# First scale and shift made in two ways, the input turned early, and eight projection groups between the modulation groups

## The chip, the core and the metric

One core of a Trainium2 chip runs the whole program. The metric is the device time of one execution in microseconds. Engines: TensorE (PE) multiplies, VectorE (DVE) and ScalarE (ACT) work elementwise, GpSimd (POOL) does small work and issues some transfers, SyncE (SP) only issues transfers, in order, and waits on semaphores in between.

## The reference

Two transformer blocks on 256 tokens of width 2048, in float32. The part at issue is the start of the first block:

```python
cond = jax.nn.silu(c)
mod = cond @ w_ada[l] + b_ada[l]
sh1, sc1, gt1, sh2, sc2, gt2 = [m[:, None, :] for m in jnp.split(mod, N_MOD, axis=-1)]
h = rms_norm(x, g_pre_mix[l]) * (1.0 + sc1) + sh1
y = token_mixing(h, w_in[l], b_in[l], ...)     # p = h @ w_in + b_in, then three branches and gates
```

`w_ada` is 2048 x 12288 and `c` one row of 2048, so `mod` is a product of one row with a 96 MB matrix. `w_in` is 2048 x 9216. The branches (spatial gating, attention with ALiBi, pooling) and twelve gate chunks are made from `p`.

## The kernel before

**Streams.** Every weight matrix is cut into groups of 1 MB (128 partitions x 4 k-tiles x 512 columns). SyncE loads them into four slots `w_raw`. For each projection group ScalarE makes a high part (`split`, L783), VectorE the rest (`split`, L1244), and TensorE does three matmuls per tile with them (`three`, L1974 to 1978): 24 matmuls of 512 columns per group for the first projection (`rows_group`, L2065). Group s uses slot s % 4; the load of group s+4 is issued when TensorE has finished group s (`pe_used`, L343 to 345). Four groups make one chunk of 512 output columns; VectorE evacuates it (`evac`, L1325).

**Front.** `N_FRONT` = 32 groups of `w_ada` (16 for the scale, 16 for the shift) go through the same four slots. TensorE multiplies them with `cond` broadcast over 128 columns (`mods`, L2041 to 2052), so every partition holds the same row of `mod`. VectorE adds the bias row, makes h1 from x in token rows (L1288 to 1303), and TensorE turns h1 (L2058 to 2061) with ScalarE and VectorE making the high and low part of `h1T` (L789, L1258). Only then the 72 groups of the first projection begin.

**Side work.** The later modulations (36 groups in this stage, `A_IN`) are summed on VectorE instead: `ada_group` (L1310) multiplies four k-tiles of 128x512 by a scalar of `cond` and adds them up; after four groups TensorE adds over the partitions (`product`, L2092) and VectorE adds the result to `mod_cols` (L1344). The loads use two slots `ada1`. On VectorE `to` (L1334) runs side group r ahead of the split of step 2(r+1); SyncE issues the load of side group r+2 in its step 2(r+1), behind the weight load of that step (L346 to 349). The branches' small steps lie between the groups by hand-written step numbers, on each engine for itself (`to(n)` runs the queue up to group n), and the bank of each turn or product follows a fixed order (`ROUNDS1`).

## Time and profile before

| | |
|---|---|
| median of 3 runs | 3100.39 us (3099.34 to 3111.67) |
| profiled execution, its own time | 3099.43 us |
| span of its trace | 3097.7 us |
| mean granted TensorE clock | 0.982 |
| TensorE matmul busy | 2986.2 us (96%) |
| VectorE busy | 1816.6 us (59%) |
| ScalarE busy | 1261.5 us (41%) |
| moved from and to memory | 215 GB/s over the span |

Times in the rows are microseconds from the span's start, and those marked ns nanoseconds. A matmul in float32 (the modulation products) leaves two records, one of the split type or a transpose leaves one. The page's part 4 gives the chain of work that ended last, followed back; its shares tell which engine the end depended on. Busy shares are means over stages with different limits, so each stage is read by itself.

### The profile page before, as it was taken

What the parts mean: (1) busy time and instruction counts of PE and PEld (TensorE: products, weight loads), DVE (VectorE), ACT (ScalarE), POOL (GpSimd) and SP (SyncE); (2) the same over time, 40 slices, a digit from 0 to 9 for tenths busy, and PEclk for the clock granted to TensorE, in tenths of its full rate; (3) what the DMA queues carried; (4) which work ended last, traced back from release to release, by engine and by line L of the source; (5) the groups of instructions that cost most, each with busy time, mean ns of one, the idle gap of its engine ahead of it and who ended that gap; (6) DMA issues with size and microseconds to landing.
All of it is one profiled execution on the core that took longest, in us unless ns stands there. A gap on an engine that the chain in (4) does not pass through costs nothing.

```text
span 3097.7 us, 43203 instructions
## 1 busy us (share of the span) xinstructions
PE 2986.2 (96%) x18072; PEld 2589.7 (84%) x18072; DVE 1816.6 (59%) x1777; ACT 1261.5 (41%) x1207; POOL 325.2 (10%) x465
## 2 busy tenths in 40 slices
PE   8899999997999999999898999998999999999998
PEld 3488777876999999888687888877889999999886
DVE  1376777787677775544455437654555555555444
ACT  0133555435444454344433434334444343443343
POOL 1000000001000000000104908720000000000000
PEclk9899999998999999999898999999999999999999
DMA  9777777885666654555546652225654555555554
GB/s 363 275 274 269 278 282 287 303 349 200 245 228 234 231 217 178 205 217 204 193 151 190 212 209 85 91 75 192 242 187 180 192 196 195 190 191 208 211 210 170
DMA packets 109853, 666.49 MB, mean 215 GB/s; under 512 B 23472, under 2 KB 25680, under 8 KB 33296
## 3 DMA queue, kind: packets, MB, share of 16 engines
q1 hardware_dynamic: 101584, 626.96, 55.8%
q0 software_dynamic: 8144, 37.74, 3.3%
q8 instruction: 94, 1.54, 0.2%
q14 instruction: 31, 0.25, 0.0%
HBM read 647.26 MB, written 17.39 MB: 215 GB/s over the span
## 4 chain that ended last, share of the span: by engine, by line
PE 91%; DVE 3%; DMA 2%; ACT 2%; issue 1%; POOL 0%; SPq 0%; DVEq 0%; ACTq 0%; POOLq 0%
PE acc L1976 27%; PE acc L1978 27%; PE acc L1977 27%; PE ms L2050 3%; PE tp L2025 1%; DVE w_lo L1244 1%; DMA ada<-ada_stream 1%; DMA w_raw<-w_stream 1%; PE ms L2435 0%; PE acc L2474 0%; DMA w_raw<-ada_stream 0%; PE acc L2464 0%; ACT w_hi L783 0%; PE ms L2434 0%; ACT bias_rows L914 0%
## 5 line engine op out<-in xcount | busy, mean ns | idle before, releaser
L1244 DVE TENSOR_TENSOR w_lo<-w_raw,w_hi 128x2048 fp32r<-128x2048 f32 x484 | 1110.0, 2303 | 731.9 <-ACT w_hi L783 713.1
L783 ACT ACTIVATE w_hi<-w_raw 128x2048 fp32r<-128x2048 f32 x484 | 922.8, 1915 | 986.1 <-DMA w_raw<-w_stream 983.8
L1976 PE MATMUL acc<-h2T_hi,w_lo 128*128 128x256 f32 x2816 | 783.0, 278 | 0.0
L1977 PE MATMUL acc<-h2T_lo,w_hi 128*128 128x256 f32 x2816 | 782.0, 278 | 0.0
L1978 PE MATMUL acc<-h2T_hi,w_hi 128*128 128x256 f32 x2816 | 781.9, 278 | 0.0
L1977 PEld LDWEIGHTS acc<-h2T_lo,w_hi 128*128 128x128 f32 x2816 | 530.7, 188 | 0.0
L1978 PEld LDWEIGHTS acc<-h2T_hi,w_hi 128*128 128x128 f32 x2816 | 530.3, 188 | 0.0
L1976 PEld LDWEIGHTS acc<-h2T_hi,w_lo 128*128 128x128 f32 x2816 | 529.7, 188 | 0.0
L1976 PE MATMUL acc<-w_hi,hid_lo 128*128 128x512 f32 x704 | 275.1, 391 | 6.1 <-DVE w_lo L1244 6.1
L1977 PE MATMUL acc<-w_lo,hid_hi 128*128 128x512 f32 x704 | 274.5, 390 | 0.0
L1978 PE MATMUL acc<-w_hi,hid_hi 128*128 128x512 f32 x704 | 274.4, 390 | 0.0
L1976 PE MATMUL acc<-w_hi,h1T_lo 128*128 128x512 f32 x576 | 231.1, 401 | 1.5 <-DVE h1T_lo L1258 1.5
L1978 PE MATMUL acc<-w_hi,h1T_hi 128*128 128x512 f32 x576 | 225.5, 392 | 0.0
L1977 PE MATMUL acc<-w_lo,h1T_hi 128*128 128x512 f32 x576 | 225.5, 391 | 0.0
L1319 DVE SCALAR_TENSOR_TENSOR mod_sum<-ada,cond,mod_sum 128x512 f32<-128x512 f32 x240 | 180.3, 751 | 42.9 <-DMA ada<-ada_stream 35.9
L1976 PEld LDWEIGHTS acc<-w_hi,hid_lo 128*128 128x128 f32 x704 | 132.5, 188 | 34.8 <-DVE w_lo L1244 7.4
L1977 PEld LDWEIGHTS acc<-w_lo,hid_hi 128*128 128x128 f32 x704 | 132.6, 188 | 27.6
L1978 PEld LDWEIGHTS acc<-w_hi,hid_hi 128*128 128x128 f32 x704 | 132.5, 188 | 27.5
L1976 PE MATMUL acc<-w_hi,nT_lo 128*128 128x512 f32 x320 | 127.7, 399 | 9.3 <-DVE w_lo L1244 9.3
L1976 PEld LDWEIGHTS acc<-w_hi,h1T_lo 128*128 128x128 f32 x576 | 108.7, 189 | 29.0 <-issue 4.5
L1978 PEld LDWEIGHTS acc<-w_hi,h1T_hi 128*128 128x128 f32 x576 | 108.7, 189 | 23.5
L1977 PEld LDWEIGHTS acc<-w_lo,h1T_hi 128*128 128x128 f32 x576 | 108.8, 189 | 21.5
(517 smaller groups left out, 3962.0 us busy)
## 6 DMA issues: line engine op xcount, KB each, us to landing
w_raw<-w_stream SPq DMA_DIRECT2D x484, 1024.0 KB, 4.8
ada<-ada_stream SPq DMA_DIRECT2D x64, 1024.0 KB, 6.9
w_raw<-ada_stream SPq DMA_DIRECT2D x32, 1024.0 KB, 4.9
g_dram<-gates_out SPq DMA_DIRECT2D x12, 512.0 KB, 7.1
gates_in<-g_dram POOLq DMA_DIRECT2D x12, 512.0 KB, 6.2
bias_rows<-b_in POOLq DMA_DIRECT2D x18, 256.0 KB, 6.1
x_res<-x POOLq DMA_DIRECT2D x2, 2048.0 KB, 12.2
g_dram<-gate_stage SPq DMA_DIRECT2D x8, 512.0 KB, 6.1
```

The costliest lines, as they stand in the source:

```text
L783: sc.activation(whi[:, s % 4], raw[:, s % 4], ACT.Copy).then_inc(hi_made, 1)
L1244: v.tensor_tensor(wlo[:, s % 4], raw[:, s % 4], whi[:, s % 4].bitcast(F32), ALU.subtract).then_inc(lo_made, 1)
L1319: chain(v.scalar_tensor_tensor(macc[:], slots[b][:, q], cond[:, k:k + 1], macc[:], ALU.mult, ALU.add))
L1976: mm(o, sl, mh, start=start, stop=False, skip_group_check=share)
L1977: mm(o, sh, ml, start=False, stop=False, skip_group_check=share)
L1978: return mm(o, sh, mh, start=False, stop=stop, skip_group_check=share)
L2025: ins = tr(t[0:w, c:c + n], src, ident[0:n, 0:n])
L2050: ins = mm(ms[n][:], cond[:, k:k + 1].to_broadcast([P, P]), raw[:, g, q], start=k == 0, stop=k == KD - 1)
```

## The change

- The 16 scale groups stay matmuls on TensorE, through four slots of their own (`ada_first`). The 16 shift groups are summed on VectorE with `ada_group` and the two slots `ada1`. SyncE issues scale and shift loads in turn, and eight projection loads (chunks 0 and 1 alternating by k-group) among them.
- x is normalized in place on VectorE (by rstd alone), turned in eight rounds on TensorE and copied by ScalarE to `xT`, while the modulations still run.
- For each quarter c of the width, ScalarE copies the scale row out of its bank, TensorE turns it to columns and adds the shift's column product in the same bank (`first_product`); VectorE adds the biases (now loaded as columns); ScalarE writes `h1T_hi` from `xT` with scale and bias as columns, VectorE the same value into `x_mod` and the difference into `h1T_lo` (`first_rows`).
- TensorE runs projection group c of chunk 0, two scale groups, group c of chunk 1, one scale group, the product, one scale group (`first_mods`, `rows_group`).
- The 36 side groups stand at the steps 10, 12, ... 70 and 17, 27, 37, 47, 57 (`SIDE`) instead of 2, 4, ... 72. The branches' steps and products move by one or two groups; of the early save of modulation rows only the first 16 rows remain.
- The broadcast loads of b_ada (2 MB) and g_pre_mix (1 MB) are replaced by loads as columns (24 KB).

```diff
+N_EARLY = 8
+SIDE = sorted(list(range(10, 71, 2)) + [17, 27, 37, 47, 57])
...
-            for j in range(4):
-                load(j, a["ada_stream"][j])
-            with sp.Fori(1, N_FRONT // 4) as i:
-                for j in range(4):
-                    sp.wait_ge(ada_used, (i - 1) * 4 + j + 1)
-                    load(j, row(a["ada_stream"], i * 4 + j))
-            for j in range(4):
-                sp.wait_ge(ada_used, N_FRONT - 3 + j)
-                load(j, a["w_stream"][j])
...
+            def first(p):
+                n, h = divmod(p, 2)
+                src = a["ada_stream"][h * 4 * GK + n]
+                if h:
+                    if n >= 2:
+                        sp.wait_ge(mod_used, n - 1)
+                    load_ada(ada1, n % 2, src)
+                else:
+                    if n >= 4:
+                        sp.wait_ge(ada_used, n - 3)
+                    sp.dma_start(adaf[n % 4][:].rearrange("p k c -> p (k c)"), src).then_inc(first_in[n % 4], 16)
+            def early(s):
+                if s >= 4:
+                    sp.wait_ge(pe_used, s - 3)
+                load(s % 4, a["w_stream"][s % 2 * 4 + s // 2])
+            for p in range(N_FRONT):
+                first(p)
+                if p >= 7 and p % 4 == 3:
+                    early(p // 4 - 1)
+            early(N_EARLY - 1)
             for j in range(2):
+                sp.wait_ge(mod_used, A_FIRST - 1 + j)
                 load_ada(ada1, j, a["ada_stream"][N_FRONT + j])
-            for s in range(G_IN1):
+            for s in range(4, G_IN1):
                 sp.wait_ge(pe_used, s + 1)
                 load(s % 4, a["w_stream"][s + 4])
-                r = s // 2 - 1
-                if s % 2 == 0 and s and r + 2 < A_IN:
-                    sp.wait_ge(mod_used, r + 1)
-                    load_ada(ada1, r % 2, a["ada_stream"][N_FRONT + r + 2])
+                for r in range(A_IN - 2):
+                    if SIDE[r] == s:
+                        sp.wait_ge(mod_used, A_FIRST + r + 1)
+                        load_ada(ada1, r % 2, a["ada_stream"][N_FRONT + r + 2])
...
-            fetch("rows1", row1[:].rearrange("p a b -> p (a b)"), bc(a["b_ada"][0]))
-            fetch("rows1", rowT1[:], bc(a["g_pre_mix"]))
             fetch("ident", ident[:], a["ident"])
+            fetch("first_cols", bcol, a["b_ada_first"])
+            fetch("first_cols", pcol, a["g_pre_mix"])
...
-            squares(lambda k: x[:, k], lambda k: h1[:, k], P, (0, 1)).then_inc(sem("ssq"), 1)
-            split()
-            split()
-            turns_hi(h1T[0], KD)
+            xflat = xT[:].rearrange("p k s -> p (k s)")
+            squares(lambda k: x[:, k], lambda k: xflat[:, k * D:(k + 1) * D], P, (0, 1)).then_inc(sem("ssq"), 1)
+            for r in range(KD // 2):
+                act.wait_ge(tp_full, r + 1)
+                sc.activation(xflat[:, r * C:(r + 1) * C], tp[r % 2][:], ACT.Copy).then_inc(tp_free[r % 2], 1)
+            for c in range(4):
+                act.wait_ge(ada_used, GK * (c + 1))
+                sc.activation(rowc[:], ms[c % 2][:], ACT.Copy).then_inc(sem("row_copied"), 1)
+                act.wait_ge(sem("mod_evac"), c + 1)
+                for k in range(GK * c, GK * c + GK):
+                    ins = sc.activation(h1T[0][:, k], xT[:, k], ACT.Identity, scale=acol[:, k:k + 1], bias=scol1[:, k:k + 1])
+                ins.then_inc(sem("h1_hi"), 1)
+                split()
+                split()
...
-            dve.wait_ge(sem("ld_rows1"), 32)
-            for n in range(2 * D // C):
-                c = slice(n % 4 * C, (n % 4 + 1) * C)
-                r = row1[:, n // 4, c]
-                dve.wait_ge(ada_used, (n + 1) * 4)
-                chain(v.tensor_tensor(r, ms[n % 2][:], r, ALU.add))
-                dve.sem_inc(sem("mod_evac"), 1)
-                if n < 4:
-                    chain(v.scalar_tensor_tensor(r, r, 1.0, rowT1[:, c], ALU.add, ALU.mult))
-                    if n == 0:
-                        rstd_wait()
-                for t in range(TT):
-                    if n < 4:
-                        chain(scaled(h1[:, t, c], x[:, t, c], t, r))
-                    else:
-                        v.tensor_tensor(h1[:, t, c], h1[:, t, c], r, ALU.add).then_inc(sem("h1"), 1)
-            split()
-            split()
-            turns_lo(h1T, KD)
...
+            def first_shifts(g0, g1):
+                for n in range(g0, g1):
+                    ada_group(ada1, macc1[n // GK % 2], n % GK)
+            def first_rows(c):
+                dve.wait_ge(sem("shifts"), c + 1)
+                k = slice(GK * c, GK * c + GK)
+                b = ms[c % 2][:].rearrange("p (f s) -> p f s", s=P)
+                v.tensor_tensor(scol1[:, k], b[:, :, 1], bcol[:, 1, k], ALU.add)
+                chain(v.tensor_tensor(acol[:, k], b[:, :, 0], bcol[:, 0, k], ALU.add))
+                chain(v.scalar_tensor_tensor(acol[:, k], acol[:, k], 1.0, pcol[:, k], ALU.add, ALU.mult))
+                dve.sem_inc(sem("mod_evac"), 1)
+                if c == 0:
+                    for b in range(2):
+                        dve.wait_ge(tp_free[b], KD // 4)
+                for i in range(GK):
+                    kk = GK * c + i
+                    ins = v.tensor_scalar(xm[:, i], xT[:, kk], acol[:, kk:kk + 1], scol1[:, kk:kk + 1], ALU.mult, ALU.add)
+                chain(ins)
+                dve.wait_ge(sem("h1_hi"), c + 1)
+                v.tensor_tensor(h1T[1][:, k], xm[:], h1T[0][:, k].bitcast(F32), ALU.subtract).then_inc(sem("h1"), 1)
+            dve.wait_ge(sem("cond"), 1)
+            first_shifts(0, GK)
+            rstd_wait()
+            for t in range(TT):
+                v.tensor_scalar(x[:, t], x[:, t], rstd[:, t:t + 1], None, ALU.mult).then_inc(sem("xn"), 1)
+            dve.wait_ge(sem("ld_first_cols"), 32)
+            for c in range(4):
+                if c < 3:
+                    first_shifts(GK * (c + 1), GK * (c + 1) + 2)
+                first_rows(c)
+                split()
+                if c < 3:
+                    first_shifts(GK * (c + 1) + 2, GK * (c + 2))
+                split()
+            dve.wait_ge(sem("h1"), 4)
...
                 while m.n <= s:
-                    r = m.n // 2 - 1
-                    if m.n % 2 == 0 and r < A_IN:
+                    if m.n in SIDE:
+                        r = SIDE.index(m.n)
                         ada_group(ada1, macc1[r // 4 % 2], r % 4)
                     split()
-                    if m.n % 4 == 2 and m.n < 4 * (BRANCH + 12) + 6:
+                    if m.n == N_EARLY + 1:
+                        evac(0)
+                    elif m.n % 4 == 2 and m.n < 4 * (BRANCH + 12) + 6:
...
+            def first_product(c):
+                pe.wait_ge(sem("row_copied"), c + 1)
+                for f in range(4):
+                    tr(ms[c % 2][:, f * P:(f + 1) * P], rowc[:, f * P:(f + 1) * P], ident[:])
+                pe.wait_ge(mod_acc, c + 1)
+                for f in range(4):
+                    ins = mm(ms[c % 2][:, f * P + 1:f * P + 2], macc1[c % 2][:, f * P:(f + 1) * P], ones[:], start=True, stop=True)
+                ins.then_inc(sem("shifts"), 1)
...
+            first_mods(0, 0, GK)
+            pe.wait_ge(sem("ones"), 1)
+            pe.wait_ge(sem("ld_ident"), 16)
+            pe.wait_ge(sem("xn"), TT)
+            for k in range(KD // 2):
+                turn([(x[:, t, (2 * k + q) * P:(2 * k + q + 1) * P], q * S + t * P) for q in range(2) for t in range(TT)])
+            first_product(0)
+            first_mods(1, 0, 2)
+            chunks.add(2)
+            for c in range(4):
+                pe.wait_ge(sem("h1"), c + 1)
+                rows_group(bank(0), h1T, c)
+                if c < 3:
+                    first_mods(c + 1, 2, GK)
+                rows_group(bank(1), h1T, c)
+                if c < 2:
+                    first_mods(c + 2, 0, 1)
+                if c < 3:
+                    first_product(c + 1)
+                if c < 2:
+                    first_mods(c + 2, 1, 2)
```

## Rows read from the trace of the kernel before

**Rows 1.** Page, part 4: the chain that ended last, share by engine.
```profile
PE 91%; DVE 3%; DMA 2%; ACT 2%; issue 1%; POOL 0%; SPq 0%; DVEq 0%; ACTq 0%; POOLq 0%
```
**Rows 2.** Windows: length, busy (records) by engine, granted clock, DMA share, GB/s.
```profile
core 0: us, PE busy (x) PEld busy (x) DVE busy (x) ACT busy (x) POOL busy (x), PEclk, DMA share, GB/s
25.00:50.00 25.00, 23.04 (x53) 10.09 (x54) 5.78 (x8) 0.00 (x0) 0.00 (x0) 1.00 0.99 397
...
125.00:150.00 25.00, 16.29 (x60) 13.06 (x61) 20.83 (x20) 7.37 (x9) 5.00 (x6) 0.66 0.65 232
```
**Rows 3.** Timeline of TensorE, front: start, length, instruction, [idle before, releaser].
```profile
30.66 92.97 PE L2050 MATMUL ms<-w_raw,cond 128*128 128x512 f32 x216 [0.26 <-DMA w_raw<-ada_stream]
123.47 1.04 PE L2025 MATMUL tp<-ident,h 128*128 128x128 f32 x8
130.95 1.94 PE L2025 MATMUL tp<-ident,h 128*128 128x128 f32 x8 [6.45 <-DVE h1T_lo L1258]
...
139.54 0.77 PE L1976 MATMUL acc<-w_hi,h1T_lo 128*128 128x512 f32 x1 [1.46 <-DVE h1T_lo L1258]
...
144.37 0.44 PE L1978 MATMUL acc<-w_hi,h1T_hi 128*128 128x512 f32 x1
```
**Rows 4.** Timeline of SyncE's queue: issues of weight and side loads.
```profile
185.67 6.72 SPq L322 DMA_DIRECT2D w_raw<-w_stream  x2
...
229.61 0.43 SPq L338 DMA_DIRECT2D ada<-ada_stream  x1
...
298.67 5.77 SPq L322 DMA_DIRECT2D w_raw<-w_stream  x2
...
310.19 5.77 SPq L322 DMA_DIRECT2D w_raw<-w_stream  x2
...
492.02 0.33 SPq L322 DMA_DIRECT2D w_raw<-w_stream  x1
...
498.11 5.77 SPq L322 DMA_DIRECT2D w_raw<-w_stream  x2
...
570.37 11.21 SPq L322 DMA_DIRECT2D w_raw<-w_stream  x3
```
**Rows 5.** All waits of TensorE from 180 to 600: us, times, longest.
```profile
PE tp L2025 <- DVEq L1348: 0.8, 1, 0.8
```
**Rows 6.** Groups by line, 140 to 600: busy us, mean ns, idle before.
```profile
L783 ACT ACTIVATE w_hi<-w_raw 128x2048 fp32r<-128x2048 f32 x75 | 143.3, 1912 | 88.9 <-DMA w_raw<-w_stream 88.8
...
L840 ACT ACTIVATE pool_y<-ms,pool_scale 128x256 f32<-128x256 f32 x4 | 1.7, 470 | 13.5 <-PE ms L2123 13.5
...
L1244 DVE TENSOR_TENSOR w_lo<-w_raw,w_hi 128x2048 fp32r<-128x2048 f32 x75 | 173.4, 2316 | 32.4 <-ACT w_hi L783 25.8 <-DVE mod_sum L1319 2.2 <-DVE mod_cols L1347 0.2
L1319 DVE SCALAR_TENSOR_TENSOR mod_sum<-ada,cond,mod_sum 128x512 f32<-128x512 f32 x135 | 101.5, 752 | 38.6 <-DMA ada<-ada_stream 34.8
...
L1440 DVE TENSOR_SCALAR scores<-scores,row_inv 128x256 f32<-128x256 f32 x8 | 2.8, 354 | 0.3
...
L1347 DVE TENSOR_TENSOR mod_cols<-mod_cols,tp 128x4 f32<-128x4 f32 x9 | 1.4, 151 | 0.0
...
L1377 DVE TENSOR_SCALAR proj<-proj,sumsq 128x512 f32<-128x512 f32 x2 | 1.0, 488 | 0.1
```
**Rows 7.** DMA issues up to 8 us: size, median us from issue to landing.
```profile
w_raw<-ada_stream SPq DMA_DIRECT2D x4, 1024.0 KB, 10.4
x_res<-x POOLq DMA_DIRECT2D x1, 2048.0 KB, 14.6
```
**Rows 8.** Windows of 4 us in the output projection, columns as in rows 2.
```profile
684.00:688.00 4.00, 1.87 (x7) 1.51 (x8) 3.93 (x4) 1.91 (x1) 0.00 (x0) 0.90 0.97 410
688.00:692.00 4.00, 4.00 (x14) 3.19 (x13) 3.78 (x5) 1.92 (x1) 0.00 (x0) 0.68 0.48 178
```
**Rows 9.** Side loads (tile ada) from 130 to 600: issue to landing.
```profile
DMA to landing us min/median/max: 6.7/7.0/10.6
```
**Rows 10.** Timeline of VectorE: the split behind a late side group.
```profile
239.73 2.29 DVE L1244 TENSOR_TENSOR w_lo<-w_raw,w_hi 128x2048 fp32r<-128x2048 f32 x1
```
**Rows 11.** Chain of waits in order of time, output projection.
```profile
667.29 9.57 DMA ada<-ada_stream
```

More of the change, by code:

```diff
@@ L197, in block_program @@
         gb1 = [u(f"gates_in{j}", [P, TT, C], 32 + 4 * j) for j in range(3)]
-        h1 = u("h1", [P, TT, D], 56)
+        adaf = [u(f"ada_first{j}", [P, GK, C], 40 + 8 * j) for j in range(4)]
+        xT = u("xT", [P, KD, S], 72)
+        xm = u("x_mod", [P, GK, S], 100)
+        rowc = u("row_copy", [P, C], 88.5)
         tril = u("tril", [P, P], 88)
-        row1, rowT1 = u("row1", [P, 2, D], 32), u("rowT1", [P, D], 48)
         y3T = [u("y3T_hi", [P, 3, 4, S], 64, F32R), u("y3T_lo", [P, 3, 4, S], 76, F32R)]
@@ L297, in block_program @@
         ada_in = [sem("ada_in0"), sem("ada_in1")]
+        first_in = [sem(f"first_in{i}") for i in range(4)]
         mod_used, mod_acc, mod_sum = sem("mod_used"), sem("mod_acc"), sem("mod_sum")
@@ L884, in _ @@
                     w = (n % 2 + 1) * P
+                    if (hp, n) == (2, 0):
+                        to(b + 4)
+                        r = R1["mod_rows1"]
+                        act.wait_ge(tp_full, r + 1)
+                        chain(sc.activation(modr1[0:D // P], tp[r % 2][0:D // P, 0:P], ACT.Copy))
+                        act.sem_inc(tp_free[r % 2], 1)
+                        act.sem_inc(sem("mod_rows"), 1)
                     to(b + 5 + 2 * n)
@@ L2038, in _, with first_mods @@
             pe.wait_ge(sem("cond"), 1)
-            modc = Tally()
-            def mods():
-                for n in range(2):
-                    if not modc.early(2):
-                        pe.wait_ge(sem("mod_evac"), modc.n - 1)
-                    for g in range(4):
-                        pe.wait_ge(raw_in[g], (modc.n + 1) * 16)
-                        for q in range(GK):
-                            k = g * GK + q
-                            ins = mm(ms[n][:], cond[:, k:k + 1].to_broadcast([P, P]), raw[:, g, q], start=k == 0, stop=k == KD - 1)
-                        ins.then_inc(ada_used, 1)
-                    modc.add()
-            mods()
-            with engine_loop(pe, N_FRONT // 8 - 1, (modc, 2)) as i:
-                mods()
-            pe.wait_ge(sem("ld_ident"), 16)
-            for n in range(4):
-                pe.wait_ge(sem("h1"), 2 * n + 2)
-                for k in range(2 * n, 2 * n + 2):
-                    turn([(h1[:, t, (2 * k + q) * P:(2 * k + q + 1) * P], q * S + t * P) for q in range(2) for t in range(TT)])
-            turned()
-            sums = Tally()
+            def first_mods(c, g0, g1):
+                if c >= 2 and g0 == 0:
+                    pe.wait_ge(sem("mod_evac"), c - 1)
+                for g in range(g0, g1):
+                    n = c * GK + g
+                    pe.wait_ge(first_in[n % 4], (n // 4 + 1) * 16)
+                    for q in range(GK):
+                        k = g * GK + q
+                        ins = mm(ms[c % 2][:], cond[:, k:k + 1].to_broadcast([P, P]), adaf[n % 4][:, q], start=k == 0, stop=k == KD - 1)
+                    ins.then_inc(ada_used, 1)
+            def first_product(c):
[6 more added lines that the diff above has]
+                ins.then_inc(sem("shifts"), 1)
             def rows_group(b, xT, g):
@@ L2073, in rows_group @@
                 end_group(ins)
+            first_mods(0, 0, GK)
[19 more added lines that the diff above has]
+                    first_mods(c + 2, 1, 2)
+            sums = Tally()
+            sums.add(GK)
             def to(s):
@@ L2126, in _ @@
             pe.wait_ge(sem("ones"), 1)
-            to(7)
-            product(0)
-            to(9)
+            to(10)
             pe.wait_ge(sem("sguw_m"), 1)
@@ L2142, in _ @@
             to(15)
-            product(1)
-            to(16)
+            product(0)
+            to(18)
             pe.wait_ge(sem("y_sgu"), 1)
@@ L2152, in _ @@
             pooled(0)
-            to(19)
+            to(21)
             pool_y(0)
-            to(20)
+            product(1)
+            to(22)
             pooled(1)
-            to(22)
+            to(23)
             pool_y(1)
-            to(23)
-            product(2)
             def qk_turn(hp):
@@ L2207, in _ @@
                     pv1(hp - 1, 3)
+                if hp == 1:
+                    product(3)
                 if hp == 3:
@@ L2212, in _ @@
                 to(b + 3)
+                if hp == 0:
+                    product(2)
                 if hp == 2:
+                    pe.wait_ge(sem("mod_cols"), 1)
+                    ring("mod_rows1")
+                    turn([(mcol[:, 0:D // P], 0)])
                     product(5)
@@ L2220, in _ @@
                     pv1(hp, n)
[L2221 to L2224 removed]
+                    if (hp, n) == (1, 1):
+                        product(4)
+                    if (hp, n) == (3, 1):
+                        product(7)
             to(64)
@@ L2228, in _ @@
             pv1(3, 3)
-            to(68)
-            pe.wait_ge(sem("mod_cols"), 1)
-            ring("mod_rows1")
-            turn([(mcol[:, 0:2 * D // P], 0)])
+            to(69)
+            product(8)
             to(71)
-            product(8)
             def merged_turns(n):
```

88 lines of the change are left out of this document (40 added, 48 removed).

## The prediction

> **What bounds the kernel now.** I read the page's chain of work first, because it tells whose time the end follows: TensorE holds 91% of it [rows 1]. So an edit is worth what it adds to or takes from TensorE's own queue. The stage windows come next [rows 2]: the first projections after 125 us are the one early stretch with TensorE far from full (16.3 of 25 us, granted clock 0.66). The timeline of TensorE says why [rows 3]. 216 records of the modulation matmuls (27 groups of 8 records) take 92.97 us, so one group of 1 MB costs 3.44 us; the DMA share is below full there, so TensorE sets this pace. Then the row is added, the input is turned, and the first projection matmul starts at 139.54. The transfer queue gives the ends of the projection groups, since each weight load is issued when a group ends [rows 4]: group 7 (the eighth) ends at 185.7, group 71 at 581.2. In between TensorE waited for others for 0.8 us in all [rows 5]. So TensorE has no slack here, and every new wait costs its full length.
>
> Call F(n) the end of group n. A projection group is 5.45 us where no small work lies between two ends: a pair of loads issued in 5.77 us, the second taking 0.33, is 5.44 apart [rows 4].
>
> **Part 1, the front.** What goes: 16 of 32 modulation groups leave TensorE (16 x 3.44 = 55.0 us), the 3 MB of broadcast rows leave the DMA engines, and the sixteen row operations on h1, hidden beside TensorE, go free. What comes: 16 multiply-add groups on VectorE, each 4 x 0.75 + 0.2 = 3.3 us [rows 6], and eight projection groups that now run inside the stage. I follow the new order by hand up to F(7).
>
> Arrivals: x lands at 16.7, and by then the transfer queue has had about four loads at half rate, the fourth at about 17.6 [rows 7]. After that one load per 2.64 us (1.05 MB at 397 GB/s) [rows 2]. The load order is scale, shift, scale, shift, so the fourth shift load (the eighth in the queue) lands at 28.2. VectorE needs 3.3 more (31.4), then normalizes x in place: two operations of 128x2048. No such row exists. From 354 ns at 256 and 488 ns at 512 elements [rows 6] the slope is 0.52 ns, so about 1.3 us each; at four times the 512 row it would be 2.0, so the bounds are 2.6 and 3.9 us. I take 2.6, since the two rows show a fixed part: 34.0.
>
> TensorE has been idle by then, so its clock is low. Eight rounds of transposes: 0.97 us each at the half clock and 0.52 at the full one [rows 3]. I take the half clock: 7.8, so 41.8. The row copy (1.2) and the first product (4 transposes and 4 one-column matmuls, taken as 2.0) bring 45.0. The next two modulation groups run cold at their start. After the gap of 6.45 us in the kernel before, matmuls were slow until 144.4, that is 4.9 us of work, half of it lost: 2.4 [rows 3]. So 45.0 + 6.9 + 2.4 = 54.3.
> The rows leave one thing open: there the slow rounds had waits of 0.65 us between them, here the eight follow each other, and if they count as work the clock could be back before the modulation groups, which takes up to 3.6 + 2.4 = 6.0 us off.
> The Trainium skill has a rule for it: TensorE: Matmul & The Clock Gate, Part 4 (PE-mode transpose), states that transposes do not count as TensorE being busy, so by it these 6.0 us are not to be had. The trace doesn't contradict it: all rounds after 130.95 stayed slow [rows 3].
>
> Now the step that repeats. Before projection group pair c can start, the product must reach VectorE: three small operations with their waits (0.9), ScalarE's four writes of h1T_hi (4 x 0.47 = 1.9), its split (1.9) and VectorE's split (2.3) [rows 6], in all 7.2 us with the signals. One modulation group (3.44) lies behind the product for c = 1 and 2, none for c = 3. So TensorE idles 3.8, 3.8 and 7.2 us. A gap of 2.4 us cost a clock of 0.90 and 0.68 in the next two 4 us windows [rows 8], 1.7 us of work lost; I take 1.6, 1.6 and, as after 6.45 us, 2.4. The sum:
> c = 0: 5.45 + 6.9 + 5.45 + 3.44 + product 1.5 + 3.44 = 26.2, from 54.4 to 80.5.
> c = 1: 3.8 + 1.6 + 26.2 = 31.6, to 112.1. c = 2: 3.8 + 1.6 + 5.45 + 6.9 + 5.45 + 1.5 = 24.7, to 136.8. c = 3: 7.2 + 2.4 + 10.9 = 20.5, to 157.3.
> Cover: the shift groups for the product of c = 3 are done about 13 us before it needs them and the loads never run dry after 50 us, so neither DMA nor VectorE's sums carry the path. F(7) comes at 157.3 in place of 185.7: a gain of 28.4 us, against the 8 groups of 5.45 (43.6) that one might book.
>
> **Part 2, the denser schedule.** Before, each of the 36 side groups (sums of the later modulations on VectorE, one every second step from 2) has its load issued four steps ahead. Now they stand at 10, 12, ... 70 and also at 17, 27, 37, 47, 57, still through two buffers. The load for side group r+2 is issued in the queue's step of side group r. So the one for step 18 is issued in step 16, after F(16); for 28 after F(26), and so at 38, 48, 58. Each step of VectorE runs side group, then split, in order; behind a late load its split waits, and behind that TensorE's group. The time from F(n) to the split: weight load issued first 0.4, landing 7.0 (6.7 to 10.6) [rows 9], sums 3.25, split 2.3, signal 0.1: 13.0 us. One such chain is in the trace: issued at 229.61, the split behind it started at 239.73 and took 2.29 [rows 4, 10]. From step n to n+2 TensorE has only group n+1 and what small work lies there.
> - Step 18: no small work is left between 16 and 18. 13.0 - 5.45 = 7.5 us.
> - Step 28: F(26) is 304.1, F(27) 310.2 (6.1), the product that moves there taken as 0.8 (eight records of a one-column matmul): 13.0 - 6.9 = 6.1.
> - Step 58: F(56) 492.0, F(57) 498.1: 13.0 - 6.1 = 6.9 [rows 4]. Step 38 as 58 (6.9), step 48 as 28 with one turn more (5.6).
> Steps 17, 27 and so on have their load three steps ahead: about 13 us against 12 to 15, at most 1 us, and it lies inside the wait that follows. Sum: 33.0 us. With it the clock falls again (gaps of 5 to 7 us, between those of 2.4 and 6.45): 2.0 us each, 10.0 for the five. Less the one wait of 0.8 [rows 5], which goes: 42.2 in all. Queued behind the waiting side group on VectorE are the split, the softmax and the bank's evacuation; they catch up before step 30.
> Edits at nothing: gelu, SGU and pooling two steps later in the same order; one row round (product and turn) earlier; no difference in work, all in TensorE's own queue as before. If a step is no longer covered, it is one small operation, below 1 us.
>
> **The sum** against the profiled execution: span 3097.7, time 3099.4, median 3100.4. 3099.4 - 28.4 + 42.2 = 3113.2; I say 3113.
>
> **Rivals.**
> A, the clock stays up: gaps and dense work in turn let it recover or never fall. For it: from 25 to 50 us TensorE was busy 23.0 of 25 us, so it had gaps, and the clock was 1.00 [rows 2]. Against: the gap of 2.4 us [rows 8]. The front gains 3.6 (rounds at 0.52) + 8.0, part 2 loses 10 less: 3113 - 21.6, about 3091.
> B, slower: the late side load lands later still. Three steps in a row now issue a weight load and a side load each. Where that happens in the kernel before, in the output projection, a side load took 9.6 us [rows 11]. If it does so here, five steps cost 2.6 more: 3126. It decides from about 7.5 us of landing, where the time passes 3116.
> C, faster: VectorE's lateness is absorbed (the load is out earlier than I read, or lands with VectorE ahead): part 2 costs nothing, 3071. Against: the order of the queue is written out, and TensorE had no slack [rows 5].
> D, the early groups don't go ahead: the queue stands at its in-order waits for VectorE's buffers, TensorE gets its eight groups only after the stage and F(7) stays near 185: 3141.
>
> **How the numbers follow.** Forecast 0.50 (own range 3103 to 3123), A 0.15, B 0.20, C 0.10, D 0.05. The range of 8 in 10 takes in A and B with the bounds of x (1.3 us) and of product and row copy (1 us each): 3088 to 3130. About 0.5%, 15.5 us, is what a measurement of this kernel can tell from no change: faster below 3085, slower above 3116. Faster is C and a tail of A: 0.12. Slower is B, D and some 0.3 of the forecast's own half: 0.40. The same 0.48.
>
> **What would show it.** F(7), read as the issue of the weight load for group 11: 157; at 146 A, at 180 D. TensorE's waits for w_lo at groups 18, 28, 38, 48, 58 of 5 to 7.5 us, each behind a side load of about 7.0 us; none is C, 9 us is B. Granted clock below 1.00 in the first 5 us after each. Between these places the groups keep 24.5 to 25 us per four. The sum is wrong at its root if the time between F(7) and F(71) is not near 438 us (395.5 before).

## The result, and the profile after

The changed kernel is slower, by a little more than a measurement of this kernel can tell from no change. One of the six runs before took 4337.0 us; the ratio is made without it.

| | before | after |
|---|---|---|
| median of the runs, us | 3099.9 (6 runs) | 3121.0 (6 runs, 3115.0 to 3125.9) |
| ratio after / before | | 1.0063, 95% interval 1.0051 to 1.0075 |
| span of the profiled execution, us | 3097.7 | 3118.4 |
| mean granted clock of TensorE | 0.982 | 0.975 |
| end of projection group 7, F(7), us | 185.7 | 156.5 |
| from there to the end of group 71, us | 395.6 | 444.8 |

The forecast was 3113, the range 3088 to 3130. The last two rows are the whole result: the front gained 29.2 us (forecast 28.4), the stretch behind it lost 49.2 (forecast 42.2), together +20.0 of the span's +20.7. They are read from SyncE's queue, as in [rows 4]; the columns are start, length and instruction. The first row is of the front and the last of the stage's end; those between stand around step 18.

```profile
123.45 49.75 SPq L330 DMA_DIRECT2D w_raw<-w_stream  x7
...
211.38 0.43 SPq L336 DMA_DIRECT2D ada<-ada_stream  x1
216.84 0.33 SPq L330 DMA_DIRECT2D w_raw<-w_stream  x1
...
232.61 0.33 SPq L330 DMA_DIRECT2D w_raw<-w_stream  x1
...
584.04 17.60 SPq L330 DMA_DIRECT2D w_raw<-w_stream  x4
```

Each weight load is issued when a group ends. The first row holds those behind groups 4 to 10: the last is issued at 123.45 + 49.75 - 0.33 = 172.9, and three groups of 5.45 ahead of it group 7 ended, at 156.5. The last row ends with the load behind group 71: 584.04 + 17.60 - 0.33 = 601.3. Group 18 ended at 232.61, 15.8 us after group 17, where a group alone takes 5.45.

The chain that ended last (page, part 4) has moved by 2% from TensorE to DMA and VectorE, against [rows 1]. The side loads hold 3% of it in the line list, where they held 1% before:

```profile
PE 89%; DVE 4%; DMA 4%; ACT 2%; issue 1%; SPq 0%; POOL 0%; DVEq 0%; ACTq 0%; POOLq 0%
PE acc L2028 27%; PE acc L2029 27%; PE acc L2030 27%; DMA ada<-ada_stream 3%; PE tp L2077 1%; DVE w_lo L1277 1%; PE ms L2101 1%; DVE mod_sum L1332 1%; DMA w_raw<-w_stream 1%; ACT w_hi L805 1%; PE ms L2509 0%; PE acc L2548 0%; PE acc L2538 0%; PE ms L2508 0%; ACT bias_rows L947 0%
```

All waits of TensorE from 160 to 620 us, where [rows 5] had a single 0.8 (columns: us in total, times, longest):

```profile
PE acc L2028 <- DVE w_lo L1277: 21.7, 7, 8.2
PE tp L2169 <- DVEq L1335: 6.8, 2, 3.7
PE ms L2245 <- ACT qkT L909: 5.0, 2, 2.5
```

Together 33.5 us. The side loads (tile ada) landed as before, so the loads are no slower as a rule (window 130 to 600 us); compare [rows 9]:

```profile
DMA to landing us min/median/max: 6.7/6.9/11.2
```

One close place in full, step 18: the side load was issued at 211.38 (above), VectorE stood idle for it and split behind it, and TensorE waited 8.21 us. Timelines of VectorE, then of TensorE:

```profile
219.41 3.11 DVE L1332 SCALAR_TENSOR_TENSOR mod_sum<-ada,cond,mod_sum 128x512 f32<-128x512 f32 x4 [7.28 <-DMA ada<-ada_stream]
222.67 4.49 DVE L1277 TENSOR_TENSOR w_lo<-w_raw,w_hi 128x2048 fp32r<-128x2048 f32 x2
```
```profile
225.02 0.79 PE L2028 MATMUL acc<-w_hi,h1T_lo 128*128 128x512 f32 x1 [8.21 <-DVE w_lo L1277]
```

From F(16) (211.0) to the split 222.67 are 11.7 us, to its end 225.0: 14.0, one more than the 13.0 of the forecast, since this load took 8.0 us to land. The granted clock (last columns: clock, DMA share, GB/s) falls in the gap and is back at 1.00 some four us after its end:

```profile
220.00:222.00 2.00, 0.00 (x0) 0.00 (x0) 1.89 (x4) 0.00 (x0) 0.00 (x0) 1.00 1.00 410
222.00:224.00 2.00, 0.00 (x0) 0.00 (x0) 1.85 (x2) 0.00 (x0) 0.00 (x0) 0.54 0.87 369
224.00:226.00 2.00, 0.98 (x2) 0.83 (x3) 2.00 (x2) 0.00 (x0) 0.00 (x0) 0.50 0.00 0
226.00:228.00 2.00, 2.00 (x6) 1.57 (x5) 1.97 (x3) 0.00 (x0) 0.00 (x0) 0.50 0.00 0
228.00:230.00 2.00, 2.00 (x8) 1.56 (x8) 1.93 (x3) 0.00 (x0) 0.00 (x0) 0.76 0.00 0
```

Busy time times the missing clock is the work lost: 0.98 x 0.5 + 2.0 x 0.5 + 2.0 x 0.24 = 2.0 us here. Summed so over all such windows from F(7) to F(71) it is 14.5 us after and none before. Waits 33.5 - 0.8 and clock 14.5 make 47.2 of the 49.2.

In the front, TensorE's timeline against [rows 3]:

```profile
35.65 6.89 PE L2077 MATMUL tp<-ident,x_res 128*128 128x128 f32 x32 [5.89 <-DVE x_res L1365]
...
45.36 10.15 PE L2101 MATMUL ms<-ada_first,cond 128*128 128x512 f32 x16
...
54.95 0.80 PE L2028 MATMUL acc<-w_hi,h1T_lo 128*128 128x512 f32 x1
```

and its waits for VectorE's split before the pairs c = 1, 2 and 3, two of 3.36 and one of 6.9:

```profile
PE acc L2028 <- DVE w_lo L1277: 13.6, 3, 6.9
```

### The profile page after: what moved, and what is told of

Same layout as the page of the kernel before. It is cut to its first block, busy times and chain, and to the rows that moved or that the text cites. A ratio compares the mean times of both kernels' runs of the same rounds, so it can differ in the third digit from the quotient of the medians.

```text
span 3118.4 us, 43026 instructions
## 1 busy us (share of the span) xinstructions
PE 2961.5 (95%) x17992; PEld 2585.1 (83%) x17992; DVE 1850.6 (59%) x1839; ACT 1271.1 (41%) x1227; POOL 325.2 (10%) x465
## 4 chain that ended last, share of the span: by engine, by line
PE 89%; DVE 4%; DMA 4%; ACT 2%; issue 1%; SPq 0%; POOL 0%; DVEq 0%; ACTq 0%; POOLq 0%
PE acc L2028 27%; PE acc L2029 27%; PE acc L2030 27%; DMA ada<-ada_stream 3%; PE tp L2077 1%; DVE w_lo L1277 1%; PE ms L2101 1%; DVE mod_sum L1332 1%; DMA w_raw<-w_stream 1%; ACT w_hi L805 1%; PE ms L2509 0%; PE acc L2548 0%; PE acc L2538 0%; PE ms L2508 0%; ACT bias_rows L947 0%
## 5 line engine op out<-in xcount | busy, mean ns | idle before, releaser
L1332 DVE SCALAR_TENSOR_TENSOR mod_sum<-ada,cond,mod_sum 128x512 f32<-128x512 f32 x300 | 225.3, 751 | 82.2 <-DMA ada<-ada_stream 73.0
L2028 PE MATMUL acc<-w_hi,h1T_lo 128*128 128x512 f32 x576 | 239.7, 416 | 35.4 <-DVE w_lo L1277 35.3
L2028 PEld LDWEIGHTS acc<-w_hi,h1T_lo 128*128 128x128 f32 x576 | 112.5, 195 | 68.4 <-issue 23.3
## 6 DMA issues: line engine op xcount, KB each, us to landing
ada_first<-ada_stream SPq DMA_DIRECT2D x16, 1024.0 KB, 10.1
```

The lines of the kernel that those rows point to most:

```text
L1332: chain(v.scalar_tensor_tensor(macc[:], slots[b][:, q], cond[:, k:k + 1], macc[:], ALU.mult, ALU.add))
L2028: mm(o, sl, mh, start=start, stop=False, skip_group_check=share)
```

## The experiments

Each kernel was timed beside the kernel before on the same chip. F(7) and F(71) are read as above; "waits" are TensorE's in the stage, from 160 to 620 us.

| kernel | median, us | before there | ratio, 95% | F(7) | F(7) to F(71) | waits |
|---|---|---|---|---|---|---|
| after | 3121.0 | 3099.9 | 1.0063 (1.0051 to 1.0075) | 156.5 | 444.8 | 33.5 |
| e1_spaced | 3077.7 | 3102.9 | 0.9919 (0.9901 to 0.9938) | 156.7 | 400.3 | 3.0 |
| e2_side_first | 3106.2 | 3102.9 | 1.0012 (1.0001 to 1.0024) | 153.4 | 432.9 | 25.3 |
| e3_old_front_close | 3135.8 | 3102.9 | 1.0098 (1.0078 to 1.0118) | 185.9 | 429.6 | 26.4 |
| e4_product_early | 3105.9 | 3102.9 | 1.0011 (0.9999 to 1.0022) | 140.0 | 442.9 | 31.3 |
| e5_filled | 3115.1 | 3101.3 | 1.0042 (1.0028 to 1.0055) | 151.8 | 447.0 | 27.3 |
| e6_spaced_early | 3063.9 | 3101.3 | 0.9881 (0.9866 to 0.9896) | 142.6 | 399.2 | 3.0 |
| e7_x_sooner | 3073.1 | 3101.3 | 0.9908 (0.9893 to 0.9923) | 145.8 | 400.8 | 3.0 |
| e8_rows_first | 3066.5 | 3100.0 | 0.9890 (0.9872 to 0.9907) | 141.7 | 404.2 | 3.0 |

**e1_spaced.** The new front is kept. Two side groups run inside it, two stand at step 8, and from 10 on they are two steps apart. The products 7 and 8 go back to their steps before, 63 and 71, and the columns of product 7 to step 66.

```diff
-SIDE = sorted(list(range(10, 71, 2)) + [17, 27, 37, 47, 57])
+SIDE = [-1, -1, 8, 8] + list(range(10, 73, 2))
...
-                for r in range(A_IN - 2):
-                    if SIDE[r] == s:
+                for r in {4: [0, 1], 6: [2], 7: [3]}.get(s, [s // 2 - 1] if s % 2 == 0 and 10 <= s <= 68 else []):
+                    if True:
...
+                else:
+                    for r in range(2):
+                        ada_group(ada1, macc1[0], r)
...
```

> The changed kernel with its new front kept and only the side groups spread out again: two run on VectorE while it waits for the last product of the front, two at step 8, and the rest every second step from 10 to 72 as in the kernel before. Theory L (the late load of the third of three close side groups costs the time, and the front by itself gains): F(7) stays at about 156.5 us, TensorE's waits for w_lo in this stage fall from 21.7 us to under 3, F(7) to F(71) goes back from 445 to about 396, and the whole is 29 us below the kernel before: about 3071. Rival V (VectorE and the DMA queue are too full once the shift sums are theirs, wherever the groups stand): the stage keeps most of its 49 us and the time stays above 3100. Rival G (the front's gain at F(7) is given back later, because the branches' steps come two groups later): F(7) at 156 but a total near 3100.

43 us below the changed kernel and 25 below before. All waits of the stage but one are gone, and that one has another cause:

```profile
PE tp L2082 <- DVE scores L1498: 3.0, 1, 3.0
```

The load behind group 7 and the last ones up to group 71 in SyncE's queue:

```profile
156.71 0.33 SPq L330 DMA_DIRECT2D w_raw<-w_stream  x1
...
546.17 11.21 SPq L330 DMA_DIRECT2D w_raw<-w_stream  x3
```

F(7) is the same (156.7), F(71) is at 557.1 in place of 601.3. So 44.5 of the 49.2 us hang on how close the side groups stand, and the front's 29 us are real: 29.0 less 4.7 is 24.3, and 25 were measured. Expected were 29 in all. What is missing is the one wait that is left, 3.0 us in group 49, and the 3.0 us of work lost by the clock around it: from F(44) to F(54) this kernel needs 68.4 us and the kernel before 62.4. Ahead of it, ScalarE's copy of the early modulation rows waits for their turn on TensorE until 404.9, behind group 47, and holds the next split. That turn is one of the steps that the change moved, counted at nothing in the forecast; no run moved it back, so this cause is read from the timelines and not tested.

**e2_side_first.** The changed kernel, with the two loads of a step in the other order.

```diff
                 sp.wait_ge(pe_used, s + 1)
-                load(s % 4, a["w_stream"][s + 4])
                 for r in range(A_IN - 2):
                     if SIDE[r] == s:
                         sp.wait_ge(mod_used, A_FIRST + r + 1)
                         load_ada(ada1, r % 2, a["ada_stream"][N_FRONT + r + 2])
+                load(s % 4, a["w_stream"][s + 4])
```

> The changed kernel with two lines of SyncE's loop exchanged: in a step that issues both, the side load goes ahead of the weight load. Theory L: the side load lands about 4.8 us after its issue instead of 7 to 8.2 and is issued 0.4 us sooner, so the third group of each of the five places comes 2.6 to 3.8 us sooner: 13 to 19 us less, 3102 to 3108. The weight load then lands late, at about 7 us, with three groups of slack. Rival V: VectorE's work is unchanged, so the time stays at 3121 within 3.

15 us below the changed kernel. The side loads landed 2.1 us sooner:

```profile
DMA to landing us min/median/max: 4.7/4.8/7.7
```

TensorE's waits in the stage fell by 8.2 (33.5 to 25.3) and the work lost by the clock from 14.5 to 10.1; the stretch is 11.9 shorter. That the late loads hold the five places is shown by this. Those five took 28.6 us to land in place of 37.7 (7.1 and 7.2 still at 38 and 58) and were issued 0.4 us sooner each. From F(n) to the end of the late split the five places took 55.4 us in place of 68.3, that is 12.9 less, about what the stretch lost. The profile is 3.1 us shorter in the front too, which the edit doesn't touch; that is a matter of the clock (last section), and as much was lost again behind F(71).

**e3_old_front_close.** The kernel before, its front untouched, with side groups at 17, 27 and 37 added in the same manner.

```diff
+SIDE = sorted(list(range(2, 67, 2)) + [17, 27, 37])
...
-                r = s // 2 - 1
-                if s % 2 == 0 and s and r + 2 < A_IN:
-                    sp.wait_ge(mod_used, r + 1)
-                    load_ada(ada1, r % 2, a["ada_stream"][N_FRONT + r + 2])
+                for r in range(A_IN - 2):
+                    if SIDE[r] == s:
+                        sp.wait_ge(mod_used, r + 1)
+                        load_ada(ada1, r % 2, a["ada_stream"][N_FRONT + r + 2])
...
-                    r = m.n // 2 - 1
-                    if m.n % 2 == 0 and r < A_IN:
+                    if m.n in SIDE:
+                        r = SIDE.index(m.n)
```

> The kernel before with one thing changed: its side groups stand at 2, 4, ... 66 and also at 17, 27 and 37, so that it has three of the five close places and the old front. Theory L: each place costs what it costs in the changed kernel, 8.8, 8.5 and 12.2 us between the same group ends, less what the last places of that kernel owe to its own order: 25 to 30 us, 3125 to 3130. Rival F (the places are late only because the new front leaves VectorE and the queue behind): no more than 5 us, 3100 to 3105.

33 us above before, with the old front: the cost doesn't need the new one. This is more than the 25 to 30 expected. By stretches: F(7) to F(24) +15.1, F(24) to F(34) +9.1, F(34) to F(44) +10.0, and from F(44) to F(67), where nothing was added, 143.0 as before. The place at 18 costs more than in the changed kernel (8.8). Here a turn stands ahead of group 17 on TensorE and needs a bank that VectorE frees only with the columns it makes after the late split of step 18 (`mod_cols(1)`), so not even group 17 runs beside the load:

```profile
PE tp L2026 <- DVEq L1349: 13.2, 1, 13.2
```

The profiled run was the slowest of four (3143.7 us against a median of 3135.8). The stage's +34.0 agrees with the median; the rest of the profile's difference is work lost by the clock behind F(71).

**e4_product_early.** The changed kernel; in the front, product(c+1) and its modulation group come ahead of the second projection group of c, so that one more group covers the hand-over to VectorE.

```diff
-                rows_group(bank(1), h1T, c)
-                if c < 2:
-                    first_mods(c + 2, 0, 1)
                 if c < 3:
                     first_product(c + 1)
+                rows_group(bank(1), h1T, c)
                 if c < 2:
-                    first_mods(c + 2, 1, 2)
+                    first_mods(c + 2, 0, 2)
```

> The changed kernel with one reordering in the front on TensorE: the product of quarter c+1 goes ahead of the second projection group of quarter c, so that this group and two modulation groups lie behind the product instead of one modulation group. Theory H (the hand-over of 7.2 us from product to the first projection group, uncovered by 3.8, 3.8 and 7.2 us, and the low clock behind it, set the length of the front): the waits at c = 1 and 2 go and the one at c = 3 falls to about 1.8 us, F(7) falls from 156.5 to about 141 and the whole by 15 us, to about 3106. Rival D (the loads set the front's length): the product then waits for the shift sums instead, F(7) stays above 152 and the time above 3117.

15 us below the changed kernel, and F(7) 16.5 earlier. The waits for VectorE's split in the front went from 13.6 to 3.0 us:

```profile
PE acc L2028 <- DVE w_lo L1277: 3.0, 2, 2.1
```

That is 10.6 us. Another 3.0 are clock behind the first product (the modulation row of 10.15 takes 7.1 here), which lie ahead of the edit and are scatter between profiles (last section). Behind the three gaps the clock had cost about 1.6 us each, 5 in all. Together that is 18.6, less some 2.4 of new short waits, most of them 0.69 us for the row copy before each later product. The stage behind it lost nothing of it (442.9).

**e5_filled.** The changed kernel with matmuls added that have no effect on the output, ahead of the groups for which TensorE waits.

```diff
+            pe.wait_ge(tp_free[0], KD // 4)
             for c in range(4):
+                for i in range([0, 4, 4, 8][c]):
+                    mm(tp[0][:], ident[:], xT[:, 2 * i:2 * i + 2].rearrange("p k s -> p (k s)"), start=True, stop=True)
                 pe.wait_ge(sem("h1"), c + 1)
...
+            to(17)
+            pe.wait_ge(tp_free[1], rounds.on_bank(1))
+            for i in range(8):
+                mm(tp[1][:], ident[:], wsT[:, 0:4].rearrange("p a b -> p (a b)"), start=True, stop=True)
             to(18)
```

> The changed kernel, with added matmuls that have no effect on the output: 4, 4 and 8 of them ahead of the first projection groups of c = 1, 2, 3 (each of 128x128 on 512 columns, at most 0.85 us cold), where TensorE idled 3 to 7 us for VectorE's split, and 8 ahead of group 18. Theory G (the low granted clock after a stall costs time of its own): the clock stays at 1.00 behind the four stalls, the stalls keep their ends, and the work behind them no longer runs at half speed: 1.6 + 1.6 + 2.4 us in the front and about 2.3 us at place 18, so about 8 us less than the changed kernel's 3121, about 3113, a ratio of about 1.004 to before; F(7) near 151 where it was 156.5. Rival N (the slow clock behind the stalls is hidden, or the added work itself runs past the stall's end): the ratio stays at 1.006 or rises to 1.008, F(7) stays at 156 or later.

Measured 6 us less, of 8 expected. In the front the price of the clock is shown clean: the pair c = 1 starts at 84.9 in both kernels, and the modulation row behind its first group at 92.08 in the changed kernel and at 90.44 here, 1.6 us sooner, the 1.6 of the forecast. The windows of the changed kernel, then of this one:

```profile
84.00:86.00 2.00, 1.10 (x4) 0.97 (x5) 1.97 (x3) 0.23 (x1) 0.00 (x0) 0.90 0.03 12
86.00:88.00 2.00, 2.00 (x6) 1.52 (x6) 1.78 (x4) 0.00 (x0) 0.00 (x0) 0.50 0.00 0
88.00:90.00 2.00, 2.00 (x8) 1.58 (x7) 1.93 (x3) 0.00 (x0) 0.00 (x0) 0.74 0.46 102
```
```profile
84.00:86.00 2.00, 2.00 (x8) 1.10 (x7) 1.97 (x3) 0.23 (x1) 0.00 (x0) 1.00 0.04 16
86.00:88.00 2.00, 2.00 (x11) 1.64 (x10) 1.78 (x4) 0.00 (x0) 0.00 (x0) 1.00 0.04 8
88.00:90.00 2.00, 2.00 (x11) 1.65 (x10) 1.93 (x3) 0.00 (x0) 0.00 (x0) 1.00 0.50 135
```

F(7) is 4.7 earlier (5.6 expected). At place 18 nothing was won: the added work ended at 219.0, TensorE stood 2.28 us all the same, and the clock fell to 0.53 and 0.62 in the next two windows of 2 us (222 to 226); a gap of that length can be enough, as in [rows 8]. The side load landed 1 us later than in the changed kernel, so group 18 took 16.5 us and not 15.8. The stage was 2.2 us longer than the changed kernel's in this profile (447.0), so that half of the front's gain was gone by F(71); the medians differ by 6.

**e6_spaced_early.** The edits of e1_spaced and e4_product_early together.

> The spaced side groups (e1_spaced, 25 us below before) and the product turned ahead of the second projection group of the front (e4_product_early, 16 us below the changed kernel) together. If the two are separate terms, as the sum has it (F(7) carries the one, F(7) to F(71) the other), they add: 3103 - 25 - 16 = 3062 us, ratio 0.987, F(7) near 140.5 and F(7) to F(71) near 396 to 399. If they share a resource (VectorE or the DMA engines, now 16 us earlier at the same rate of loads), the second part lengthens: side loads then find the queue less drained, and up to the 16 us come back: 3062 to 3078.

The best kernel of the study, 37 us below before. F(7) is 142.6 and the stretch 399.2: the stage keeps all its gain. The front keeps 14.1 of e4's 16.5. The two edits alone make 25 and 15 us, so 3 us less than their sum were measured, which the intervals don't tell from nothing. The two side groups that e1 put into the front are the edit that lies there, but this wasn't split further.

**e7_x_sooner.** As e6, and x is normalized one shift group sooner.

```diff
-            first_shifts(0, GK)
+            first_shifts(0, GK - 1)
             rstd_wait()
             for t in range(TT):
                 v.tensor_scalar(x[:, t], x[:, t], rstd[:, t:t + 1], None, ALU.mult).then_inc(sem("xn"), 1)
+            first_shifts(GK - 1, GK)
```

> As e6_spaced_early, and VectorE normalizes x after the third shift group of the front, not after the fourth. In the changed kernel the transposes of x began at 35.65 us, behind that fourth group's load. If the front's chain is the one told (shift load, sums, x, turns, product, projection), the turns begin about 5.3 us sooner (two loads of 2.64 us), at about 30.4, and what follows the product keeps its lengths: 5 us less than e6_spaced_early, about 3057. The limit: the fourth shift load is then also the last thing that the first product needs, at 33 to 37 us plus the product (1.5 us), and the turns take 5 to 7 us beside it; so 2 to 5 us less. If the front's end is set by the later loads, no difference (within 2 us).

5 us less were expected and 9 more measured: the expectation was wrong. The turns did begin at 29.8, and the product was done by 37.5, 7 us sooner. Yet VectorE took it up no sooner, since the sums of the next two shift loads stand ahead of it in its queue, each waiting for its load. VectorE in this kernel (the trace calls the columns of scale and shift conv_taps, and the last row is the first operation on the product):

```profile
37.70 0.49 DVE L1330 TENSOR_SCALAR mod_sum<-ada,cond 128x512 f32<-128x512 f32 x1 [4.87 <-DMA ada<-ada_stream]
38.22 2.33 DVE L1332 SCALAR_TENSOR_TENSOR mod_sum<-ada,cond,mod_sum 128x512 f32<-128x512 f32 x3
42.49 3.12 DVE L1332 SCALAR_TENSOR_TENSOR mod_sum<-ada,cond,mod_sum 128x512 f32<-128x512 f32 x4 [1.94 <-DMA ada<-ada_stream]
45.75 0.16 DVE L1347 TENSOR_TENSOR conv_taps<-ms,conv_taps 128x4 f32<-128x4 f32 x1
```

In e6 the last of these stands at 45.85. So TensorE's time from 37.5 on turned into a wait: 6.42 us before the first projection group, where e6 has 1.16. And the wait cost the clock. TensorE's first projection record in e7, then in e6:

```profile
52.62 0.76 PE L2034 MATMUL acc<-w_hi,h1T_lo 128*128 128x512 f32 x1 [6.42 <-DVE w_lo L1277]
```
```profile
52.71 0.47 PE L2033 MATMUL acc<-w_hi,h1T_lo 128*128 128x512 f32 x1 [1.16 <-DVE w_lo L1277]
```

Both start within 0.1 us; the modulation row behind the group starts at 60.92 and at 58.26. That difference, 2.7 us, is what a gap of 6.4 us costs in clock against one of 1.2, and it is most of the 3.2 us by which F(7) is later. The span grew by 9.0. Of this 4.2 lie behind F(71), where no edit is: the waits there are the same as in e6, but the work lost by the clock is about 30 us and not about 24. Why the clock is lower there stays open; the medians show the 9 us too.

**e8_rows_first.** As e7, and for c = 0 VectorE makes the product's operations and the first split ahead of those two sums.

```diff
-                if c < 3:
+                if 0 < c < 3:
                     first_shifts(GK * (c + 1), GK * (c + 1) + 2)
...
-                    first_shifts(GK * (c + 1) + 2, GK * (c + 2))
+                    first_shifts(GK * (c + 1) + (2 if c else 0), GK * (c + 2))
```

> As e7_x_sooner, and for c = 0 VectorE makes the product's three small operations, x_mod, h1T_lo and the first split before the sums of the next two shift loads, not behind them. In e7_x_sooner the product was turned by 37.5 us, 7 us earlier than in e6_spaced_early, and yet VectorE took it up at 45.75 in place of 45.85, since it stood behind two shift loads (sums at 37.70 and 42.49, each waiting for its load); TensorE's stall before the first projection group grew from 1.2 to 6.4 us and its clock fell, so that F(7) came at 145.8 and not 142.6. If that order is the cause of the miss, the product is taken up at about 37.8 here, the first projection group starts at about 45, and F(7) comes 5 to 8 us before that of e6_spaced_early (135 to 138): about 3057 us, ratio 0.986. The rival: the next loads, now freed later (VectorE sums shift loads 5 and 6 only from about 45 us), hold product(1) back, F(7) stays at 141 or later, and the time is e6_spaced_early's 3064 or above.

The order was what held e7 back: the product is taken up at 38.16 and the first pair starts at 45.02, 7.7 us sooner. But the rival is what came. The next shift loads are freed later, and the next product waits for them. VectorE's last shift sum and product of c = 1 in e8, then in e6:

```profile
70.25 3.11 DVE L1332 SCALAR_TENSOR_TENSOR mod_sum<-ada,cond,mod_sum 128x512 f32<-128x512 f32 x4 [2.61 <-DMA ada<-ada_stream]
73.51 0.16 DVE L1347 TENSOR_TENSOR conv_taps<-ms,conv_taps 128x4 f32<-128x4 f32 x1
```
```profile
68.44 3.11 DVE L1332 SCALAR_TENSOR_TENSOR mod_sum<-ada,cond,mod_sum 128x512 f32<-128x512 f32 x4 [2.02 <-DMA ada<-ada_stream]
71.70 0.16 DVE L1347 TENSOR_TENSOR conv_taps<-ms,conv_taps 128x4 f32<-128x4 f32 x1
```

In both VectorE waited for the load ahead of this product (2.61 and 2.02 us), so there the loads set the front, and the product comes 1.8 us later than in e6. From 46 to 50 us, with the buffers freed late, the DMA engines were busy for only half of the time in e8 and all of it in e6. The 7.7 us are gone. F(7) is 0.9 earlier, group 8 then waited 3.2 us for its accumulator bank, and F(71) is 4.2 later than in e6.

## Why the prediction was right, and where its steps were off

The sign, the size and both mechanisms were as forecast; the time was 8 us above, inside the range. The forecast drew its line for "slower" at 3116 and gave that 0.40, and 0.48 to no change that can be told; the median lies above the line.

**The front, step by step.** Turns start at 35.65 (34.0 for the end of x's two operations, which took 2.48 together and not 2.6; they began at 33.02, since the fourth shift load came about 1.4 us later than by the even rate of loads). The rounds took 6.9 and not 7.8. The two cancel: the modulation row after the product starts at 45.36 (forecast 45.0), the first projection group at 54.95 (54.4). The waits were 3.4, 3.4 and 6.9 (3.8, 3.8, 7.2), F(7) 156.5 (157.3). The clock's price of a short gap was taken from [rows 8] as 1.7 us over whole windows; busy time times the missing clock is 1.5 there, and e5 measured 1.6. Rival D would have had 185; it fell.

**The five close places.** TensorE's waits sum to 33.5 us (33.0 forecast), by place 8.2, 5.3, 6.5, 5.8 and 7.7 (7.5, 6.1, 6.9, 5.6 and 6.9). Two errors cancel in this. From F(n) to the end of the late split the five took 14.0, 13.3, 14.2, 13.0 and 13.8 us, 3.3 more in all than five times 13.0. And TensorE's own work in between was longer by 2.8 in all, most of it at 28 and 38, where a part of it ran at the low clock (1.7 us lost at 38).

Not foreseen was where the waits stand. Two of 2.5 us are for ScalarE's qk copy, behind groups 36 and 56, and 1.1 and 1.3 us for the splits of steps 27 and 47. They come from the side groups put in at 27, 37, 47 and 57. ScalarE at step 37: the gate of the bank before stands ahead of the copy, and waited for VectorE's evacuation, which stands behind the sum of step 37 and its split:

```profile
355.86 1.06 ACT L853 ACTIVATE gates_out<-gates_out 128x1024 f32<-128x1024 f32 x1 [10.05 <-DVE gates_out L1384]
...
357.35 0.39 ACT L909 ACTIVATE qkT<-tp 128x256 f32<-128x256 f32 x1
```
```profile
357.88 0.46 PE L2245 MATMUL ms<-qkT 64*128 64x128 f32 x2 [2.54 <-ACT qkT L909]
```

The step that was off is the one that said steps 17, 27 and so on cost at most 1 us "inside the wait that follows". They do lie inside it: all four stand between F(n) and the end of the late split, so the waits at the splits of 38 and 58 are 3.9 and 5.3 us and not 6.9. But they are longer than 1 us, two of them through a second engine, and at 38 they cost clock. In e2, where the side loads land sooner, the waits for the qk copy are gone.

**The mis-sized term is the clock.** Taken as 2.0 us for each place, 10.0 in all; it was 14.5, or 2.9 each. By place it was 2.0, 2.8, 4.7, 2.9 and 2.1. At 38 it fell twice, at the qk wait and at the split, which the forecast had as one gap; at 58, behind a qk wait of 2.4 us, it didn't fall until the split. This is the largest part of the 7 us by which the stretch was longer than forecast.

**By stretches**, each place's price after against before: F(7) to F(24) 8.8 us (forecast 9.5 for place 18), F(24) to F(34) 8.5 (8.1), F(34) to F(44) 12.2 (8.9), F(44) to F(54) 8.8 (7.6), F(54) to F(67) 9.9 (8.9); another 1.0 lies between F(67) and F(71). Place 38 is the outlier. Its side load took 8.2 us from issue (355.75) to the sum's start (363.96), yet its waits were 6.5, below the forecast's 6.9; what came on top is the clock, 4.7 in place of 2.0.

**The rivals.** A (the clock stays up) fell: 14.5 us were lost in the stage, and e5 and e7 show the price of single gaps (1.6 and 2.7). B (9.6 us of landing) fell as a rule, with a median of 6.9. But the five late loads took 8.0, 7.0, 8.2, 6.8 and 7.7, 7.5 on the mean, which is where the forecast said that the time would pass 3116. C (absorbed) fell, by the 33.5 us of waits.

**The rule on transposes.** The eight rounds now follow each other, which the rows of before left open. The granted clock:

```profile
38.00:40.00 2.00, 2.00 (x11) 1.57 (x9) 1.89 (x4) 1.39 (x3) 0.00 (x0) 0.50 1.00 422
40.00:42.00 2.00, 1.88 (x11) 1.33 (x10) 0.46 (x1) 1.39 (x4) 0.00 (x0) 0.69 1.03 434
42.00:44.00 2.00, 0.82 (x7) 0.59 (x8) 1.54 (x3) 1.49 (x3) 0.00 (x0) 1.00 1.00 422
44.00:46.00 2.00, 2.00 (x13) 1.84 (x12) 1.78 (x5) 0.00 (x0) 0.00 (x0) 0.66 1.02 430
46.00:48.00 2.00, 2.00 (x3) 0.67 (x2) 1.46 (x5) 1.83 (x4) 0.00 (x0) 0.50 1.01 426
```

It rose to full speed by 42 us, with nothing but transposes run since the gap that ended at 35.65; in e2_side_first and e4_product_early it was at 1.00 from 40 us on. The Trainium skill (TensorE: Matmul & The Clock Gate, Part 4, PE-mode transpose) says that a transpose does not count as TensorE being busy in the same way, and that the full clock doesn't come with it. The float32 transposes measured here disagree with that. The time nearly agreed all the same, and that was luck: in this execution the clock fell again by 46 us and the modulation groups ran cold, as forecast for another reason (the gap before the transposes). In e2 and e4 they ran at full speed, and the first projection group started at 52.63, 2.3 us sooner.

## What to carry to other kernels

Before a queue of side work is packed closer, write down for each item when its load is issued and not only when it is used: with two buffers the load of item r+2 leaves at item r, and one item put between two others takes its lead from four steps to two. Work that moves ahead keeps its gain only if the schedule behind it keeps its spacing; here the same front was worth 25 us with the old spacing and cost 21 with the closer one. And when an engine's wait is shortened from one side, look at once at what stands in the queue of the engine that hands over: e7 and e8 took some 7 us off one step and got none of it.

## What the runs showed of the hardware

The same front can run with different clocks. In the changed kernel and in e5_filled, the 16 modulation records behind the first product took 10.15 and 10.10 us, at a granted clock of 0.50 from 46 to 50 us. In e2_side_first, e4_product_early and e6_spaced_early, with the same code up to there, they took 7.11, at 1.00 throughout, and in e1_spaced 8.50, at 0.50 to 48 us and 0.96 to 50. The turns had started at 35.65 and 35.67 in the first two and at 35.67 in e1, at 35.78, 35.74 and 35.86 in the three fast ones. So up to 3.0 us in the front of any single profile of this kernel are a matter of when the clock comes back, and differences of that size between two profiles need the medians.

The order of two loads of 1 MB issued one behind the other is worth 2.1 us to the one that goes first: a median of 4.8 us to landing against 6.9 (side loads in e2_side_first and in the changed kernel).
